# A decoder block on eight cores: contraction slices outside, token pieces inside, from the mixer on

## The reference

```
u = rmsnorm(h)
z = u @ w_in                     # gates: gate_a, gate_b = sigmoid(... + b_gate), 2048 wide each
y_conv = (zb * causal_dwconv3(zc * zv)) @ w_conv_out          # contraction 1024
y_mla  = causal_block_attention(q, k, v) @ w_mla_out          # contraction 2048
h = h + (gate_a * y_conv + gate_b * y_mla) @ w_o              # the mixer and w_o
u = rmsnorm(h)
a = causal_dwconv3(u @ w_ffn_up) + bias                       # 2 x 5632 wide
h = h + (silu(a_gate) * a_up) @ w_ffn_down                    # contraction 5632
```

## Time and profile before

| | us |
|---|---|
| median of 3 runs (2415.24 to 2418.70) | 2418.13 |
| the profiled execution, its own time | 2421.73 |
| its span on the slowest core, core 2 | 2419.1 |
| TensorE busy on core 2 | 2353.7 |
| VectorE busy on core 2 | 1341.8 |
| ScalarE busy on core 2 | 1094.4 |

### The profile page before, as it was taken

The page is one execution under the profiler, slowest core; times in us unless marked ns, Lnnn a source line. Parts: engine busy times, 40 slices in busy tenths (PEclk is TensorE's granted clock), DMA queues, the critical chain, the costliest instruction groups (busy, mean ns, idle before and its releaser), DMA issues.

```text
span 2419.1 us, 41786 instructions; the slowest of 8 cores (2397.2 to 2419.1 us)
## 1 busy us (share of the span) xinstructions
PE 2353.7 (97%) x13851; PEld 1245.3 (51%) x13900; DVE 1341.8 (55%) x2585; ACT 1094.4 (45%) x1877; POOL 172.6 (7%) x330
## 2 busy tenths in 40 slices
PE   4989999999999999999999999999999999999999
PEld 3874555555555555544444444444444444444444
DVE  3872777777777777761111112277457457547742
ACT  5953788888788878861111113333023113213310
POOL 1000000000000000000000000000100100110011
PEclk9999999999999999999999999999999999999999
DMA  9753121202020202144544457454554454455467
GB/s 221 167 97 64 20 40 24 40 19 50 14 50 14 50 10 50 49 98 90 83 80 82 83 125 170 70 88 76 77 93 80 73 92 81 73 90 87 78 111 153
DMA packets 65893, 188.34 MB, mean 78 GB/s; under 512 B 7616, under 2 KB 23232, under 8 KB 64512
## 3 DMA queue, kind: packets, MB, share of 16 engines
q0 software_dynamic: 46944, 140.56, 36.1%
q1 hardware_dynamic: 18720, 44.91, 5.6%
HBM read 310.20 MB, written 13.66 MB: 134 GB/s over the span
## 4 chain that ended last, share of the span: by engine, by line
PE 95%; DMA 2%; DVE 1%; ACT 1%; issue 1%; SPq 0%; ACTq 0%; DVEq 0%; POOLq 0%
PE ps L621 95%; ACT arena L628 1%; DMA arena<-wkvin 1%; DMA arena<-wall 1%; DVE arena L639 1%; DVE arena L635 0%; SPq L655 0%; ACT L628 0%; ACTq L187 0%; DVEq L187 0%; DVE arena L1098 0%; DVE arena L652 0%; POOLq L187 0%; SPq L187 0%
## 5 line engine op out<-in xcount | busy, mean ns | idle before, releaser
L621 PE MATMUL ps<-arena 128*128 128x476 bf16 (+7 forms) x13851 | 2353.7, 331 | 61.0 <-ACT arena L628 34.4
L621 PEld LDWEIGHTS ps<-arena 128*128 128x128 bf16 x13900 | 1245.3, 98 | 1169.1 <-issue 83.3
L639 DVE TENSOR_TENSOR arena<-ps,arena 128x476 f32<-128x476 f32 (+6 forms) x558 | 329.7, 591 | 776.3 <-PE ps L621 754.0
L639 DVE TENSOR_TENSOR arena<-arena 128x478 f32<-128x478 f32 (+18 forms) x1292 | 640.0, 536 | 196.2 <-ACT arena L628 174.0
L628 ACT ACTIVATE arena<-arena 128x476 f32<-128x476 f32 (+9 forms) x543 | 378.5, 712 | 683.8 <-DVE arena L639 607.6
L628 ACT ACTIVATE arena<-ps,arena 128x476 bf16<-128x476 f32 (+6 forms) x832 | 490.9, 631 | 410.2 <-PE ps L621 377.1
L635 DVE SCALAR_TENSOR_TENSOR arena<-arena 128x476 f32<-128x476 f32 (+8 forms) x603 | 358.2, 609 | 45.5 <-ACT arena L628 24.2
L628 ACT ACTIVATE arena<-ps 128x512 bf16<-128x512 f32 (+7 forms) x496 | 267.6, 561 | 117.5 <-PE ps L621 114.9
L655 POOL DMA_DIRECT2D arena<-wall x302 | 159.3, 528 | 2117.1 <-PE ps L621 2070.1
L635 DVE SCALAR_TENSOR_TENSOR arena<-ps,arena 128x256 bf16<-128x256 f32 (+1 forms) x65 | 27.1, 464 | 12.0 <-PE ps L621 7.3
L655 POOL DMA_DIRECT2D arena<-xg x23 | 12.5, 560 | 101.3 <-ACT arena L628 57.3
(11 more groups left out here) (3 smaller groups left out, 0.3 us busy)
## 6 DMA issues: line engine op xcount, KB each, us to landing
arena<-wall POOLq DMA_DIRECT2D x182, 512.0 KB, 5.5
arena<-wall POOLq DMA_DIRECT2D x48, 320.0 KB, 4.3
arena<-xg SPq DMA_DIRECT2D x9, 1024.0 KB, 6.9
arena<-wall POOLq DMA_DIRECT2D x32, 256.0 KB, 3.8
arena<-xg POOLq DMA_DIRECT2D x15, 512.0 KB, 10.2
arena<-xo SPq DMA_DIRECT2D x16, 477.0 KB, 13.8
outT<-arena SPq DMA_DIRECT2D x31, 238.0 KB, 5.3
arena<-wall POOLq DMA_DIRECT2D x32, 224.0 KB, 5.7
```

Source lines behind the costliest of these rows:

```text
L621: S.add(PE, lambda e: e.matmul(out, lhsT=lhsT, rhs=rhs, start=start, stop=stop), reads, writes, cost=max(width(rhs) / 2400.0, 0.055) + 0.003)
L639: S.add(DVE, lambda e: e.tensor_tensor(out=out, in0=in0, in1=in1, op=op), reads, writes, cost=dcost(out, in0, in1) + held)
```

## The change

Everywhere from the mixer on, the loop over pieces goes inside the loop over slices: one block of weights is used for two or three matmuls in a row, into two or three banks that are taken ahead of the loop. The evictions of the group follow its last matmul. In the w_o stage pieces 0 and 1 go together and piece 2, where there is one, alone. `mt1` and `yg` get a slab for each piece. In `up`, all pieces of `fg` come before those of `fu`, and `fg` is freed after its own group. In the last products g = 3 and g = 4 each go over all pieces, except in the last block (c = 15), which stays piece by piece.

```
# mixer
             w, Tw = wget((key, c))
+            p = [bank(8) for _ in T3]
+            for k in range(16):
+                for t, (off, n) in enumerate(T3):
+                    mm(PS[p[t]][:, 0:n], w[:, k, :], u_own[:, k, 2 + off:2 + off + n], k == 0, k == 15, [Tw] + Tup[k],
+                       [TP[p[t]]])
...
# w_o stage
         w, Tw = wget(("wo", c))
+        ps = {}
         for t, (off, n) in enumerate(T3):
-            p = bank()
-            for k in range(16):
-                mm(PS[p][:, 0:n], w[:, k, :], mT[:, k, off:off + n], k == 0, k == 15, [Tw, Tm[k]], [TP[p]])
+            if t != 1:
+                ts_ = [t, 1] if t == 0 else [t]
+                for x in ts_:
+                    ps[x] = bank()
+                for k in range(16):
+                    for x in ts_:
+                        mm(PS[ps[x]][:, 0:T3[x][1]], w[:, k, :], mT[:, k, T3[x][0]:T3[x][0] + T3[x][1]], k == 0, k == 15,
+                           [Tw, Tm[k]], [TP[ps[x]]])
+            p = ps[t]
             tt(hres[:, c, off:off + n], PS[p][:, 0:n], hres[:, c, off:off + n], ALU.add, [TP[p], Th[c]], [Th[c]])
...
# up(j)
+        for gi, key, A__, y_, Ty_, jc in ((0, "fg", Ag, yg, Tyg, j), (1, "fu", Au, yu, Tyu, 44 + j)):
+            w, Tw = wget((key, j))
+            p = [bank(8) for _ in T3]
+            for k in range(16):
+                for t, (off, n) in enumerate(T3):
+                    mm(PS[p[t]][:, 0:n], w[:, k, :], u2[:, k, off:off + n], k == 0, k == 15, [Tw, Tu2[k]], [TP[p[t]]])
+            wdone((key, j))
...
# down(g) and the last products
-    def products(g, c, p, o, n, start, stop):
+    def products(g, c, ps, os_, start, stop):
         w, Tw = wget(("fd", g, c))
         for jj in range(FG[g]):
             s = (FO[g] + jj) % NFT
-            mm(PS[p][:, 0:n], w[:, jj, :], fT[:, s, o:o + n], start and jj == 0, stop and jj == FG[g] - 1,
-               [Tw, TfT[s]], [TP[p]])
+            for p, (o, n) in zip(ps, os_):
+                mm(PS[p][:, 0:n], w[:, jj, :], fT[:, s, o:o + n], start and jj == 0, stop and jj == FG[g] - 1,
+                   [Tw, TfT[s]], [TP[p]])
...
-        for o, n in os_:
-            p = bank(8)
+        for group in [os_] if c < 15 else [[x] for x in os_]:
+            pg = [bank(8) for _ in group]
             for g in (3, 4):
-                products(g, c, p, o, n, g == 3, g == 4)
-            out(c, p, o, n)
+                products(g, c, pg, group, g == 3, g == 4)
+            for p, (o, n) in zip(pg, group):
+                out(c, p, o, n)
```

More of the change, by code:

```diff
@@ L1677, in share_program @@
     sgb, Tsgb = P5.slabs(NT, [W], F32, "sgb")
-    mt1, Tmt1 = P5.slabs(2, [W], F32, "mt1")
+    mt1, Tmt1 = P5.slabs(NT, [W], F32, "mt1")
     mt2, Tmt2 = P5.slabs(2, [W], F32, "mt2")
@@ L1682, in share_program @@
             w, Tw = wget((key, c))
+            p = [bank(8) for _ in T3]
[3 more added lines that the diff above has]
+                       [TP[p[t]]])
             for t, (off, n) in enumerate(T3):
-                p = bank(8)
-                for k in range(16):
-                    mm(PS[p][:, 0:n], w[:, k, :], u_own[:, k, 2 + off:2 + off + n], k == 0, k == 15, [Tw] + Tup[k], [TP[p]])
-                act(dst[:, t, 0:n], PS[p][:, 0:n], AF.Sigmoid, [TP[p], Tcst], [Td[t]], bias=C("bgate", bo + c))
+                act(dst[:, t, 0:n], PS[p[t]][:, 0:n], AF.Sigmoid, [TP[p[t]], Tcst], [Td[t]], bias=C("bgate", bo + c))
             wdone((key, c))
@@ L1690, in share_program @@
         wmo, Twmo = wget(("mo", c))
+        p = [bank(8) for _ in T3]
+        for k in range(8):
+            for t, (off, n) in enumerate(T3):
+                mm(PS[p[t]][:, 0:n], wco[:, k, :], gcv[:, k, off:off + n], k == 0, k == 7, [Twco, Tgc[k]], [TP[p[t]]])
+        for t, (off, n) in enumerate(T3):
+            tt(mt1[:, t, 0:n], PS[p[t]][:, 0:n], sga[:, t, 0:n], ALU.mult, [TP[p[t]], Tsga[t]], [Tmt1[t]])
+        p = [bank(8) for _ in T3]
+        for k in range(16):
+            for t, (off, n) in enumerate(T3):
+                mm(PS[p[t]][:, 0:n], wmo[:, k, :], attnT[:, k, off:off + n], k == 0, k == 15, [Twmo, Tat[k]], [TP[p[t]]])
         for t, (off, n) in enumerate(T3):
             x = t % 2
[L1693 to L1701, removed]
+            tt(mt2[:, x, 0:n], PS[p[t]][:, 0:n], sgb[:, t, 0:n], ALU.mult, [TP[p[t]], Tsgb[t]], [Tmt2[x]])
+            tt(mT[:, c, off:off + n], mt1[:, t, 0:n], mt2[:, x, 0:n], ALU.add, [Tmt1[t], Tmt2[x]], [Tm[c]])
         wdone(("co", c))
@@ L1747, in share_program @@
         TA.append([S.region(o + off * 4, n * 4, "A") for off, n in T3])
-    yg, Tyg = PF.slabs(2, [W], F32, "yg")
+    yg, Tyg = PF.slabs(NT, [W], F32, "yg")
     yu, Tyu = PF.slabs(2, [W], F32, "yu")
@@ L1756, in up @@
             wget((key, j))
[L1757 to L1768, removed]
+        for gi, key, A__, y_, Ty_, jc in ((0, "fg", Ag, yg, Tyg, j), (1, "fu", Au, yu, Tyu, 44 + j)):
+            w, Tw = wget((key, j))
+            p = [bank(8) for _ in T3]
+            for k in range(16):
+                for t, (off, n) in enumerate(T3):
+                    mm(PS[p[t]][:, 0:n], w[:, k, :], u2[:, k, off:off + n], k == 0, k == 15, [Tw, Tu2[k]], [TP[p[t]]])
+            wdone((key, j))
+            for t, (off, n) in enumerate(T3):
+                x = (j * NT + t) % 2 if gi else t
+                lo = max(off - 2, 0)
+                m = off + n - 2 - lo
+                tt(A__[:, off:off + n], PS[p[t]][:, 0:n], rstd2[:, t, 0:n], ALU.mult, [TP[p[t]], Trstd2[t]], [TA[gi][t]])
                 rd = [TA[gi][t], Tcst] + ([TA[gi][t - 1]] if t else [])
@@ L1772, in up @@
                 settle()
-                late.append((gi, y, A__, lo, m, jc, rd, Ty_[x], x, j))
+                late.append((gi, y, A__, lo, m, jc, rd, Ty_[x], x, j, t))
     def settle():
@@ L1778, in settle @@
             return
-        gi, y, A__, lo, m, jc, rd, Ty, x, j = late.pop(0)
+        gi, y, A__, lo, m, jc, rd, Ty, x, j, t = late.pop(0)
         stt(y, A__[:, lo + 1:lo + 1 + m], C("fcw", 3 * jc + 1), y, ALU.mult, ALU.add, rd + [Ty], [Ty])
@@ L1784, in settle @@
         else:
-            tt(fT[:, j % NFT, lo:lo + m], yg[:, x, 0:m], y, ALU.mult, [Tyg[x], Ty], [TfT[j % NFT]])
-    def products(g, c, p, o, n, start, stop):
+            tt(fT[:, j % NFT, lo:lo + m], yg[:, t, 0:m], y, ALU.mult, [Tyg[t], Ty], [TfT[j % NFT]])
+    def products(g, c, ps, os_, start, stop):
         w, Tw = wget(("fd", g, c))
@@ L1790, in products @@
             s = (FO[g] + jj) % NFT
-            mm(PS[p][:, 0:n], w[:, jj, :], fT[:, s, o:o + n], start and jj == 0, stop and jj == FG[g] - 1,
-               [Tw, TfT[s]], [TP[p]])
+            for p, (o, n) in zip(ps, os_):
+                mm(PS[p][:, 0:n], w[:, jj, :], fT[:, s, o:o + n], start and jj == 0, stop and jj == FG[g] - 1,
+                   [Tw, TfT[s]], [TP[p]])
     def down(g):
         for c in range(16):
-            for o, n in sh.O:
-                p = bank(8)
-                products(g, c, p, o, n, True, True)
+            ps = [bank(8) for _ in sh.O]
+            products(g, c, ps, sh.O, True, True)
+            for p, (o, n) in zip(ps, sh.O):
                 hh = hres[:, c, 2 + o:2 + o + n]
@@ L1825, in share_program @@
         for c in range(npre):
-            for t, (o, n) in enumerate(sh.O):
-                products(g, c, ps[c][t], o, n, g == 3, g == 4)
-                if g == 4:
+            products(g, c, ps[c], sh.O, g == 3, g == 4)
+            if g == 4:
+                for t, (o, n) in enumerate(sh.O):
                     out(c, ps[c][t], o, n)
```

## The result

The change made the kernel slower: ratio to the kernel before 1.0138, 95% interval 1.0121 to 1.0156. The profiled execution took 2450.75 us, the other one that counts 2451.99, about 33 us more than the 2418.1 of before; the forecast was 2443.6, 25.5 more, in a range of 2433 to 2453.

The account below looks back on a forecast made before the run. TensorE on the slowest core, core 2, was taken to bound the kernel. The w_o stops' +27.0 us and the last products' -1.5 gave +25.5, taking the median from 2418.1 to 2443.6 us, range 2433 to 2453.

Parts of the forecast that it names:

- The w_o stop: w_o stage, two-piece cores: TensorE waits each block for piece 0's eviction and square before its stat; 27.0 us on core 2.
- late restart of 0.19 us a block: w_o stage: after each stat the first product starts 0.39 us later, against 0.20 undisturbed; 16 x 0.19 = 3.0 us.
- The last products: Last products, core 2: more slack for weight blocks shrinks the stops for weights; -1.5 us (0 to -1.9).
- A load taken away or left makes no step shorter: All TensorE steps: repeated weight loads save 0, bound 2 ns per repeated step; load count stays about 13,900.
- the 64 matmuls in 3.40 us: Attention-stage projections: 128-column matmuls, each with its load, read as 53 ns a step, showing no time for the load.
- part (1): Mixer, `up`, `down`: evictions come in bursts but clear within the next group; cost 0, else 0.65 us a group.
- 499 steps in 100 us of `up`, unchanged: `up`, core 2: sign of being right, the matmul count in 100 us stays as before the change.
- Within 1 us of before: Spans of three-piece cores 0 and 1: sign of being right, only the two-piece cores pay.
- Rival B: Steps repeating weights get shorter from the mixer on; +18 us at the 2 ns bound, 2411 at 10 ns; chance 0.03.
- C: Rival: no change, the w_o stop hidden because stops elsewhere shrink as much; 2418 us, chance 0.02.
- E: Rival: eviction bursts hold TensorE in `up` or `down`, a bank coming free late; up to 57 us, chance 0.05.
- D: Rival: w_o stops halve the clock at each block; up to 52 us (2495), one drop 3 us; chance 0.04.

Follow-up runs that it names:

- e4: Kernel before, in mixer and `up` slices k and k+1 both use the even slice's weights; no time given, core 2 1493 matmuls in 300 us (before 1494).
- e12: Changed kernel with stats issued one group late and pieces in falling order in all stages from the mixer on; median 2418.4 us, ratio to before 0.9997.
- e2_wo_only: Kernel before with only the change's w_o loop; median 2444.35 us against 2416.65, ratio 1.0117.
- e3: Changed kernel, in mixer and `up` each piece's slices offset, weights and tokens together, so neighbours' weights differ; core 1 at 2410.9 us.
- e5: Changed kernel, in mixer and `up` every matmul of a group streams piece 0's tokens; no time given, core 2 1490 matmuls in 300 us (after 1483).
- e11: Changed kernel, in mixer and `up` the pieces of a slice in falling order; no time given, core 2 1491 matmuls in 300 us (after 1483).
- e6b: Changed kernel, in mixer and `up` all matmuls of a group summed into one bank; no time given, core 2 1483 matmuls in 300 us, like after.
- e9: Changed kernel, in mixer and `up` only the weights' slice offset per piece, streamed slice kept; no time given, core 2 1483 matmuls in 300 us, like after.

## Why the prediction was right, and where it was wrong

- **The w_o stop: right in place, chain and price.** Forecast 2.09 us from the last matmul of piece 0 to its stat, 27.0 us in all on core 2. Measured: 16 stops, one a block, 1.32 us idle in the typical one, and a last one at the end of the stage. With 0.165 for the record's tail, the two steps since the last matmul of piece 0 (0.40) and the older stat's step (0.20) that is 2.08. The sum was 24.9 net, 2.1 less than forecast. The term that was too large is the late restart of 0.19 us a block, which I carried over from the end of the stage to all blocks: 15 x 0.19 = 2.9 us. Three stops longer than the typical one by 0.3 us each gave part of it back.
- **The last products: right.** Forecast -1.5, bound -1.9; the idle time went to nothing after the change.
- **"A load taken away or left makes no step shorter", loads stay 13,900: right**, by the profile's page and by e4 and e12, which repeat weights and have the step of before. One reading behind it was off by the same counting of records that reach into a window: the 64 matmuls in 3.40 us include three that began ahead of them. The timeline of that run on core 3 has 42 in 2.51 us; less the last one's record of 0.219 these are 41 steps of 55.9 ns, not 53:

```profile
265.71 2.51 PE L621 MATMUL ps<-arena 128*128 128x128 bf16 x42
```

That is 2.6 ns over the 53.3 of its columns, about as much as the steps of 476 columns have over theirs (201.0 ns, not 200.4, against 198.3). A load that cost time would show more in the shorter step, so what the prediction drew from the run stands.

- **"Only the order on TensorE moves", part (1), cost 0: wrong, +9.8 us on core 2.** The "499 steps in 100 us of `up`, unchanged" were 496. I weighed the new order for banks, evictions and loads, and took the step's 2 ns over N / 2.4 GHz as something that could only shrink. The order of the streamed addresses was not on the list. It is also what moved the three-piece cores. Core 0 from the first matmuls after its last stat wait (1309.69 before, 1306.84 after) to the end: 1095.9 and 1106.4 us, +10.5 for two thirds of its steps. "Within 1 us of before" for cores 0 and 1 was wrong for that reason. None of the signs of being wrong that the prediction listed was a longer step.
- **Rival B (+18 at the most) and C**: nothing in the runs speaks for them. **E**: no stop ended by VectorE in `up` or `down`. **D**: through the 16 single stops the clock stayed at 1.00, but after the two stops in a row that end the stage it was at half for a short time; two windows of core 2, over the blocks of w_o and from inside the last stop on (at 1590 to 1600 it is 1.00 again):

```profile
1456.00:1583.00 127.00, 106.24 (x511) 49.47 (x509) 19.65 (x30) 35.50 (x60) 7.92 (x15) 1.00 0.45 93
1586.50:1589.50 3.00, 2.33 (x6) 0.96 (x7) 0.00 (x0) 2.96 (x4) 0.00 (x0) 0.50 0.67 134
```

The window of 3 us at half clock is worth 1.5 us. It doesn't follow each time: in e2_wo_only core 2 has the same two stops (1.32 and 1.78 us idle, one matmul between them) and full clock behind them, and so it is in e3 and e5:

```profile
1585.00:1588.00 3.00, 2.43 (x12) 1.19 (x13) 0.00 (x0) 2.88 (x5) 0.00 (x0) 1.00 0.88 164
```

The half clock at the mixer's start was shorter than before by about as much (0.83 over 1082 to 1092 against 0.66 over 1084 to 1094), so that the two about cancel in the +32.8.

The measured times, 2451.4 us on average, lie 7.8 us above the forecast of 2443.6: the longer step (+9.8) was missing, the w_o sum was 2.1 too high, and the last products gave 0.4 more than forecast. (Between the profiled spans the miss is only 4.6 us, +30.1 against +25.5, since the code ahead of the change happened to be 2.7 us faster in the profiled run after.) That the time still fell into the range is in part luck: its upper end had room for a longer chain at each block, no gain in the last products and one or two drops of the clock. Of these only one drop came, worth 1.5 us; the rest of the room was taken up by a cost that the prediction didn't have. For the loss on the three-piece cores it had no mechanism at all.

**What stays open.** Why a stream that goes on where the last one ended takes 1 to 2 ns longer. e11 shows that the order of the addresses decides; which part of the machine it is, and whether exact adjacency or only a short forward way is needed, was not tried. (In `up` the 478 and 476 columns of the two pieces fill a slab of 954, so pieces and slices lie back to back; in the gates two columns lie between slices, and the mixer's count fell too.) Two of the 16 stops (1.67 and 1.60 us of idle at blocks 1 and 5) were longer than the typical one and came back in other runs, such as e3; why was not followed up. Nor was why the clock fell after the last two stops in some runs and not in others.

## What to carry to other kernels

When products are grouped, look in each engine's own order for what had been issued "one product late": grouping shortens that distance, and a wait that was covered by a product stands bare. Ask whether the weight load shows in the step at all before reordering for it: a run of short matmuls tells (its steps by their starts, not by a count over a short window). And in a kernel that TensorE bounds, count the matmuls of a fully busy stretch before and after; 1.5 ns a step is invisible in any mean duration and was 10 us here.

## What the runs showed of the hardware that was not expected

- The step of a matmul depends on where its streamed operand lies against the one before: 201.0 ns when it jumps, 202.5 when it goes on (476 and 478 columns), 180.8 against 181.9 (428), 151.4 against 153.0 (358 and 356), from the counts above. Other banks, other weights and their repetition changed no count by more than one (e4, e6b, e9).
- A repeated stationary operand costs no less than a new one: 1984 against 1983 matmuls in 300 us on core 1 in e12 and before.
- One TensorE stop of 1.3 us every 8.4 us left the granted clock at 1.00 (after, 1456 to 1583). Two in a row, of 1.3 and 1.8 us with one matmul between, were followed by a stretch at half in some runs (after, e12) and by full clock in others (e2, e3, e5).
